# Seven products of a Strassen-Winograd matrix: three of them added up in PSUM, the relu moved to ScalarE, rstd applied behind the second matrix

## The reference, cut to what matters

```python
h = h + jnp.concatenate([y_rw, y_fox], axis=-1) @ w_out[i]
u = rmsnorm(h, norm_mlp[i])
h = h + jnp.square(jax.nn.relu(u @ w_ff1[i])) @ w_ff2[i]
gate = jax.nn.sigmoid(rmsnorm(h, norm_ple[i]) @ w_ple_gate[i])
```

## Time and profile before

| | us |
|---|---|
| median of 3 runs | 2773.17 (2772.51 to 2775.59) |
| the profiled execution | 2775.37 |
| its span, first to last instruction | 2773.8 |
| PE busy in the span | 2591.0 (93%) |
| VectorE | 1698.0 (61%) |
| ScalarE | 1031.7 (37%) |
| GpSimd | 565.3 (20%) |
| mean granted TensorE clock | 0.986 of full speed |

### The profile page before, as it was taken

The page is one execution under the profiler, slowest core; times in us unless marked ns, Lnnn a source line. Parts: engine busy times, 40 slices in busy tenths (PEclk is TensorE's granted clock), DMA queues, the critical chain, the costliest instruction groups (busy, mean ns, idle before and its releaser), DMA issues.

```text
span 2773.8 us, 48519 instructions
## 1 busy us (share of the span) xinstructions
PE 2591.0 (93%) x18322; PEld 2104.7 (76%) x18322; DVE 1698.0 (61%) x2030; ACT 1031.7 (37%) x1458; POOL 565.3 (20%) x389
## 2 busy tenths in 40 slices
PE   8999999999688998898999899879999999999998
PEld 5777777777577676677777777768888888888887
DVE  5565667666444645899999999973333333333443
ACT  4444444444455334333333333332222222233333
POOL 0000000000232025544444444410000000011010
PEclk9999999999899999999999999989999999999999
DMA  6555554555423334333333333364444444333333
GB/s 196 152 151 158 156 147 138 147 153 163 166 92 112 103 116 129 107 121 113 113 113 113 113 114 118 121 207 116 126 121 121 116 119 127 100 93 109 93 97 107
DMA packets 469436, 352.24 MB, mean 127 GB/s; under 512 B 56661, under 2 KB 435527, under 8 KB 468359
## 3 DMA queue, kind: packets, MB, share of 16 engines
q1 hardware_dynamic: 413111, 281.93, 35.1%
q0 software_dynamic: 11472, 39.43, 4.1%
q10 hardware_dynamic: 44800, 30.18, 3.3%
HBM read 294.21 MB, written 57.28 MB: 127 GB/s over the span
## 4 chain that ended last, share of the span: by engine, by line
issue 36%; PE 33%; DVE 20%; ACT 4%; POOL 3%; DMA 2%; SPq 1%; ACTq 1%; DVEq 0%; POOLq 0%
DVE w_lo L2296 8%; PE acc L682 7%; PE acc L684 6%; PE acc L683 6%; DVE tile_sums L2300 2%; DVE ev L2347 2%; PE bank L1188 2%; ACT w_hi L1285 1%; ACT w_hi L1677 1%; PE bank L1189 1%; DVE sq L2350 1%; POOL sumsq L2501 1%; PE bank L870 1%; POOL sumsq L2622 1%; ACT sq L1682 1%
## 5 line engine op out<-in xcount | busy, mean ns | idle before, releaser
L1815 DVE TENSOR_TENSOR w_lo<-w_raw,w_hi 128x1024 fp32r<-128x1024 f32 x292 | 361.2, 1237 | 760.9 <-ACT w_hi L1285 760.0
L1285 ACT ACTIVATE w_hi<-w_raw 128x1024 fp32r<-128x1024 f32 x292 | 308.7, 1057 | 791.3 <-PE acc L684 744.3
L1188 PE MATMUL bank<-mix,w_hi 128*128 128x512 f32 x1120 | 410.8, 405 | 62.1 <-DVE w_lo L2296 62.1
L682 PE MATMUL acc<-hidden,w_hi 128*128 128x512 f32 x1024 | 399.7, 390 | 15.6 <-DVE w_lo L1815 11.5
L684 PE MATMUL acc<-hidden,w_lo 128*128 128x512 f32 x1024 | 399.4, 390 | 0.0
L683 PE MATMUL acc<-hidden,w_hi 128*128 128x512 f32 x1024 | 399.3, 390 | 0.0
L682 PE MATMUL acc<-a_all,w_hi 128*128 128x512 f32 x800 | 321.7, 402 | 2.0 <-DVE w_lo L1815 2.0
L1189 PE MATMUL bank<-mix,w_lo 128*128 128x256 f32 x1120 | 314.9, 281 | 0.0
L684 PE MATMUL acc<-a_all,w_lo 128*128 128x512 f32 x800 | 313.1, 391 | 0.0
L683 PE MATMUL acc<-a_all,w_hi 128*128 128x512 f32 x800 | 312.8, 391 | 0.0
L1188 PEld LDWEIGHTS bank<-mix,w_hi 128*128 128x128 f32 x1120 | 212.2, 189 | 131.0 <-issue 49.7
(11 more groups left out here) (358 smaller groups left out, 4493.4 us busy)
## 6 DMA issues: line engine op xcount, KB each, us to landing
parts<-in_w_ff SPq DMA_DIRECT2D x64, 1024.0 KB, 5.8
w_raw<-in_w_ff SPq DMA_DIRECT2D x128, 512.0 KB, 3.9
w_raw<-in_w_in SPq DMA_DIRECT2D x100, 512.0 KB, 3.9
w_raw<-in_w_out SPq DMA_DIRECT2D x32, 512.0 KB, 4.0
hid_d<-sq ACTq DMA_DIRECT2D x32, 512.0 KB, 2.6
w_raw<-in_w_ple_gate SPq DMA_DIRECT2D x32, 512.0 KB, 4.0
z_d<-ev POOLq DMA_DIRECT2D x50, 256.0 KB, 3.4
ev<-hid_d SPq DMA_DIRECT2D x24, 512.0 KB, 4.5
```

What stands on the lines that cost most here:

```text
L682: mm(dst, wh, hi[kt], start=kt == 0, stop=False)
L1188: mm(dst[:, :], wh[:, j, :], mixed(u, j), start=j == 0, stop=False, skip_group_check=True)
L1285: A(w_hi[:, s, :, :], w_raw[:, s ^ raw_turned[0], :, :], ACT.Copy).then_inc(sg("w_hi_ready"), 1)
L1815: V.tensor_tensor(w_lo[:, s, :, 0:width], w_raw[:, s ^ raw_turned[0], :, 0:width], w_hi[:, s, :, 0:width].bitcast(F32), ALU.subtract).then ...
```

## The change

**PSUM.** The seven products keep their operands. Their order and their banks change. From pair 1 on: b11 into bank 0, b21 into bank 1, bt2 onto bank 0, bt1 into bank 2, bt3 onto bank 0, b22 onto bank 2, bt4 into bank 4. Before a product is added onto a bank, VectorE has read what stood there, since the partial sums are needed too. Pair 0 has a table of its own.

**VectorE.** Four reductions stay (`take_first`, `take_16`, `take_fifth`, `take_167`). The other three become two adds each that take a half of the bank straight from PSUM. Relu and rstd leave VectorE: ScalarE does the relu ahead of its square (`store_hidden`), and rstd, squared, multiplies the second matrix's result (`grow_second`, two instructions where `grow` was one).

**GpSimd and SP.** bt2 is made second and bt3 third; the two halves of the weights are loaded later in the pair than before.

**Seams.** In the output projection's loop ScalarE makes the high part of the weights ahead of scaling. GpSimd makes bt1 of pair 0 ahead of the last tile's sums. At the end SP loads the weights of the second matrix's tile 1 ahead of the wait for the last hidden store, and the second half of h is loaded two tiles later.

```diff
+
+    A11, A12, S2, S1, S3, S4, A22 = range(UNITS)
+    FIRST_PAIR = ((b11, A11, bank[0], True), (b21, A12, bank[1], True), (b22, S4, bank[2], True), (bt1, S1, bank[5], True),
+                  (bt2, S2, bank[0], False), (bt3, S3, acc[0], True), (bt4, A22, bank[4], True))
+    LATER_PAIR = ((b11, A11, bank[0], True), (b21, A12, bank[1], True), (bt2, S2, bank[0], False), (bt1, S1, bank[2], True),
+                  (bt3, S3, bank[0], False), (b22, S4, bank[2], False), (bt4, A22, bank[4], True))
+    LATER_TURN = (1, 2, 3, 0, 4, 5, 6)
+
+    def pair_order(p):
+
+        return FIRST_PAIR if p == 0 else LATER_PAIR
+
+    def turn_of(p, u):
+
+        return LATER_TURN[u] if p > 1 else u
 
     Z_ODD = 2
...
+                    sp.wait_ge(sg("weight_sums_made"), i * 4 + (past("weight_sums_made") + a + 3))
                     sp.sem_inc(sg("waits_taken"), 1)
-                    sp.wait_ge(sg("w_split"), i * UNITS + (FIRST + 2 * a + 3))
+                    sp.wait_ge(sg("w_split"), i * UNITS + (FIRST + 4 * a + 4))
...
             second_units(0, 0, 0)
             for q in range(4, UK):
                 load_staged(q)
-            sp.wait_ge(sg("relu_ready"), past("relu_ready") + PAIRS)
+            second_units(0, 0, 1)
+            sp.wait_ge(sg("hidden_relu"), past("hidden_relu") + PAIRS)
             sp.wait_ge(sg("hidden_stored"), past("hidden_stored") + 16 * PAIRS)
-            second_units(0, 0, 1)
             stage_hidden(1, 0)
...
+                    pe.wait_ge(sg("w_split"), i * UNITS + (FIRST + UNITS * p + max(turn_of(p, v) for v in range(u + 1)) + 3))
+                    if p == 0:
+                        if u == 4:
+                            pe.wait_ge(sg("products_taken"), past("products_taken") + 1)
+                        if u == 5:
+                            pe.wait_ge(sg("acc_taken"), M_FF + 1)
+                    elif u == 6:
+                        pe.wait_ge(sg("hidden_summed"), i + (past("hidden_summed") + p))
+                    else:
+                        pe.wait_ge(sg("products_taken"), i * 6 + (past("products_taken") + 6 * (p - 1) + (5, 2, 7, 6, 9, 10)[u]))
...
                             pe.wait_ge(sg("mix_split"), past("mix_split") + 3 * NJ + (2 if u == 2 else 3))
-                        mm(dst[:, :], wh[:, j, :], mixed(u, j), start=j == 0, stop=False, skip_group_check=True)
-                        last = mm(dst[:, 0:HT], wl[:, j, :], mixed(u, j)[:, 0:HT], start=False, stop=j == NJ, skip_group_check=True)
+                        mm(dst[:, :], wh[:, j, :], mixed(x, j), start=fresh and j == 0, stop=False, skip_group_check=True)
...
+                hi_unit(0, i, M_OUT + KT // 2 + 1, a_turn=1)
                 scale_tile(i, 0, 0)
                 square_tile(i, 0, 0)
-                hi_unit(0, i, M_OUT + KT // 2 + 1, a_turn=1)
+                hi_unit(1, i, M_OUT + KT // 2 + 1, a_turn=1)
...
+                if p == 0:
+                    act.wait_ge(sg("squares_summed"), 2 + 2 * KT)
                 else:
-                    freed = FIRST + 2 + UNITS * p + (u - 2 if u < 3 else u - 6 if u == 3 else u - 3)
-                act.wait_ge(sg("unit_done"), i * UNITS + freed)
-                A(slots[slot_of[u]][0], weights_of[u], ACT.Copy).then_inc(sg("w_hi_ready"), 1)
-
-            def square_hidden(i, p):
-
-                act.wait_ge(sg("relu_ready"), i + (past("relu_ready") + p + 1))
+                    act.wait_ge(sg("hidden_stored"), i * 16 + (past("hidden_stored") + 16 * p))
+                A(sq[:, :, :], ev[:, :, :], ACT.Relu).then_inc(sg("hidden_relu"), 1)
+                act.wait_ge(sg("hidden_relu"), i + (past("hidden_relu") + p + 1))
                 A(sq[:, :, :], sq[:, :, :], ACT.Square).then_inc(sg("hidden_squared"), 1)
                 act.wait_ge(sg("hidden_squared"), i + (past("hidden_squared") + p + 1))
                 act.dma_start(hid_d[bass.ds(i + p, 1), :, :, :].rearrange("a p b t -> (a p) b t"), sq[:, :, :]).then_inc(sg("hidden_stored"), 16)
...
+                lo_unit(1, i * 2 + (OUT_U + 3))
                 mix_los(i, 0, 0)
-                lo_unit(1, i * 2 + (OUT_U + 3))
...
-            def sums_76(i, p):
+                    V.reduce_sum(sum_167, halves_of(bank[0]), AX.X).then_inc(sg("products_taken"), 1)
...
-                take_product(pq[3], 4)
-                take_product(pq[4], 5).then_inc(sg("products_taken"), 1)
-                taken(i, p, 3)
-                then(V.tensor_tensor(pq[4], pq[0], pq[4], ALU.add))
-                V.tensor_tensor(ev[:, 1, 0:HT], pq[4], pq[1], ALU.add)
-                V.tensor_tensor(pq[3], pq[3], pq[4], ALU.add)
-
-            def sums_4(i, p):
+                then(V.tensor_tensor(ev[:, 1, 0:HT], bank[2][:, 0:HT], sum_16, ALU.add))
+                if p == 0:
+                    then(V.tensor_tensor(ev[:, 1, 0:HT], ev[:, 1, 0:HT], fifth, ALU.add))
+                V.tensor_tensor(ev[:, 1, 0:HT], bank[2][:, HT:T], ev[:, 1, 0:HT], ALU.add).then_inc(sg("products_taken"), 1)
+
+            def sum_21(i, p):
 
                 await_product(i, p, 6)
-                dve.wait_ge(sg("w_split"), i * UNITS + (FIRST + UNITS * (p + 1) + 1 + 3))
-                take_product(pq[1], 6).then_inc(sg("products_taken"), 1)
-                taken(i, p, 4)
-                then(V.tensor_tensor(ev[:, :, HT:T], pq[3][:, None, :].broadcast_to([P, 2, HT]), tile_sums[:, 1:3, :], ALU.add))
-                if p:
-                    dve.wait_ge(sg("hidden_stored"), i * 16 + (past("hidden_stored") + 16 * p))
-                V.scalar_tensor_tensor(sq[:, :, :], ev[:, :, :], 0.0, rstd[:, None, :].broadcast_to([P, 2, T]), ALU.max, ALU.mult).then_inc(
-                    sg("relu_ready"), 1)
+                then(V.tensor_tensor(ev[:, 0, HT:T], bank[4][:, 0:HT], sum_167, ALU.add))
+                V.tensor_tensor(ev[:, 0, HT:T], bank[4][:, HT:T], ev[:, 0, HT:T], ALU.add).then_inc(sg("hidden_summed"), 1)
+
+            def begin_pair(i, p):
+
+                take_first(i, p)
+                product_lo(i, p, 4)
+                sum_11(i, p)
+                product_lo(i, p, 5)
+                take_16(i, p, 3, 2)
+                product_lo(i, p, 6)
+                take_fifth(i, p, 3)
 
...
+            mean_square(1)
+            sum_21(0, 0)
+            product_lo(0, 1, 2)
+            product_lo(0, 1, 3)
+            invert_root(1)
+            begin_pair(0, 1)
+            then(V.tensor_tensor(rstd[:, :], rstd[:, :], rstd[:, :], ALU.mult))
             with dve.Fori(0, PAIRS - 2) as i:
-                end = chained(i, 2)
-                sums_35(i, 1)
+                end = chained(i, 3)
+                product_lo(i, 2, 3)
+                take_167(i, 1, 4)
+                sum_22(i, 1)
                 product_lo(i, 2, 0)
-                sums_76(i, 1)
+                sum_12(i, 1)
                 product_lo(i, 2, 1)
-                to_last_lo(i, 2, lambda: sums_4(i, 1))
+                sum_21(i, 1)
+                product_lo(i, 2, 2)
+                begin_pair(i, 2)
...
+            def grow_second(i, b, n):
+
+                V.tensor_tensor(grown_part[:, b, :], acc[b][:, :], rstd[:, :], ALU.mult).then_inc(sg("acc_taken"), 1)
+                dve.wait_ge(sg("acc_taken"), 2 * i + (n + b + 3))
+                return V.tensor_tensor(h2[:, bass.ds(2 * i + b, 1), :], h2[:, bass.ds(2 * i + b, 1), :], grown_part[:, b:b + 1, :], ALU.add)
...
             pool.wait_ge(sg("unit_done"), FIRST + 2 + UNITS * PAIRS)
             for n in range(2):
+                if n:
+                    pool.wait_ge(sg("unit_done"), FIRST + 2 + UNITS * PAIRS + 4)
```

More of the change, by code:

```diff
@@ L385, in build @@
     slot_of = (0, 1, 2, 3, 0, 1, 2)
[L386 to L388 removed]
+    b11, b12, b21, b22 = parts[:, 0, :, 0:P], parts[:, 0, :, P:], parts[:, 1, :, 0:P], parts[:, 1, :, P:]
+    bt1, bt2, bt3, bt4 = (tsum[:, n, :, :] for n in range(4))
+    A11, A12, S2, S1, S3, S4, A22 = range(UNITS)
[8 more added lines that the diff above has]
+        return LATER_TURN[u] if p > 1 else u
     Z_ODD = 2
```

274 lines of the change are left out of this document (141 added, 133 removed).

## The result

The changed kernel takes 2714.14 us (median of 4 runs, 2709.24 to 2714.75); the kernel before, run between them, 2774.38. The ratio is 0.9778, 95% interval 0.9761 to 0.9795: faster by 60 us, where 109 were forecast.

| stretch | before, us | after, us | difference | forecast |
|---|---|---|---|---|
| to the projection's last matmul | 1106.93 | 1091.21 | -15.7 | -14.5 |
| from there to the last step of pair 1 | 58.13 | 64.54 | +6.4 | -5.5 |
| the other 30 pairs | 676.4 (22.55 a pair) | 636.8 (21.23) | -39.6 | -72.6 |
| from there to the end | 932.3 | 920.7 | -11.7 | -16 |

What follows compares the result with a forecast made beforehand. VectorE, 98.5% busy, was taken to set the pace, PE some 3 us behind. Terms -14.5 - 5.5 - 71.6 - 1 - 16 = -108.6 took the profiled 2775.4 to 2666.8, as median 2664.6; prediction 2665, range 2645 to 2706.

Steps and rivals of the forecast that it cites:

- The pairs: Loop over column-tile pairs of the first MLP matrix: 20.1 us a pair instead of 22.57, saving 71.6 us.
- PE's floor: First MLP matrix: seven products of 2.78 us need 19.5 us a pair on PE.
- rival 2: Loop over pairs: PE alone sets the pace, 19.5 us a pair, a further -17, kernel 2647; chance 0.20.
- the 0.6 us wait at product 6: Loop over pairs: PE waits once a pair, at product 6, for the third reduction, losing 0.6 us.
- VectorE's work: Loop over pairs: VectorE's work falls from 16.2 to 13.2 us a pair, its port-bound part from 11.6 to 8.3.
- Rival 1: Loop over pairs: GpSimd keeps the port over back-to-back sums 2 and 3; 21.45 us a pair, kernel 2704; chance 0.20.
- Projection: Output projection: ScalarE's high part of the weights goes first, removing PE's waits; -14.5 us.
- Start: First two pairs after the projection: early sum 1 lets product 4 start sooner; -5.5 us, bounds 0 and -12.
- Seam: Passage to the second matrix: tile 1's weight loads issued before the last store's wait; -16 us, bounds -8 and -18.

Runs made afterwards that it cites:

- x2: Changed kernel with one wait more: GpSimd's sum 2 of a pair waits for the low part of that pair's product 1; 2703.7 us, ratio 0.9741.
- x3: Changed kernel with VectorE's add of two SBUF inputs (sum of a22) moved behind the low part of the next pair's product 1; 2710.4 us, ratio 0.9766.
- x9: Changed kernel with b11's low and high parts (product 1) ahead of bt1's (product 4) in the loop over the pairs; 2674.8 us, ratio 0.9646.
- x4: Changed kernel with the order of the output projection's loop restored on ScalarE and VectorE; 2728.8 us, ratio 0.9824.
- x1: Changed kernel with the second reciprocal and the squaring of rstd moved behind the loop over the pairs; 2710.7 us, ratio 0.9764.
- x11: x9 plus x1's change, with pair 1's low part for product 4 behind the reduction that product 3 waits for; 2667.9 us, ratio 0.9620.
- x7: Changed kernel with the first pair's sum 1 back behind the last tile's sums on GpSimd; 2720.0 us, ratio 0.9793.
- x13: x11 with VectorE's wait for h moved from ahead of the second matrix's loop to the add that uses it; 2671.1 us, ratio 0.9633.
- x5: Changed kernel with the loads for tile 1 of the second matrix behind the last relu and store waits again; 2723.2 us, ratio 0.9814.

## Why the prediction was wrong, step by step

**The pairs: the step that failed.** The prediction placed one pair and had it close at 20.1 us; it measured 21.23. It closed with "low part 1 to 17.75" and "sum 2 gets the port at 17.75". It also had the weights for sum 2 land at 16.35, under the add that lasts to 16.6, and low part 1 ask only at 16.6: sum 2 had asked first, and I gave the port to the other all the same. The trace follows the placing to 0.5 us up to there and then decides it the other way. With product 1 starting at 1177.2, sum 1 starts at 10.7 (placed 10.25), sum 2 is released and runs at 16.6 (16.35), low part 1 asks at 16.7 and waits (16.6). What repeats is two pairs, one short (19.0 to 20.2) and one long (22.8 to 23.9). x2 shows that the alternation goes when the add and low part 1 are both ahead of sum 2, x3 that low part 1 alone is not enough; x9 shows that the loss goes altogether when VectorE's queue no longer holds product 1's part behind product 4's. That order stood in the diff, and I placed "low part 4 of the next pair" ahead of low part 1 without asking what it holds up when it is late. It is late where sum 1 is: with the order at the port fixed (x2) sum 1 runs at 13.1 of its pair (1436.34, product 1 from 1423.3) and not at 10.25. Its load is asked for at 5.5, behind a sum 3 that I had done by 3.6, and lands 7.4 us later, where I took 5.8.

**PE's floor: a term mis-sized.** I took 2.78 us a product from the earlier trace rows, hence 19.5. Most undisturbed products take 2.83, in the changed kernel's loop (110 of 173) as in before's (74 of 121), and a pair of them 19.79; rival 2's 19.5 was never to be had at that pace. Over the 30 pairs that is 9 us, and the 0.6 us wait at product 6 would have stood on top of it. There was no such wait: PE waits at products 1, 2, 3 and 5.

**VectorE's work** was right in size: the adds with a PSUM operand take 0.41 to 0.43 us and are never stretched, reductions 0.68 to 0.69. The group rows of 1200 to 1780 us, to be held against the earlier trace rows:

```profile
L2328 DVE TENSOR_TENSOR w_lo<-parts,w_hi 128x1024 fp32r<-128x1024 f32 x82 | 162.5, 1981 | 3.2 <-ACT w_hi L1699 3.2
L2381 DVE TENSOR_TENSOR ev<-tile_sums 128x256 f32<-128x256 f32 x27 | 27.3, 1010 | 0.9
...
L2394 DVE TENSOR_TENSOR ev<-bank,tile_sums 128x256 f32<-128x256 f32 x28 | 11.5, 412 | 0.0
```

The one 256-wide add without a PSUM operand (L2381) takes 1010 ns on average, its equal from PSUM 412. By the Trainium skill (SBUF — State Buffer, "Who interferes with whom") VectorE's instructions contend with GpSimd's reads if they have two SBUF inputs and, outside the two-port modes, not if they have one at most. The trace agrees.

**Rival 1** came close in size (21.45 a pair, 2704) and not in kind: GpSimd did not keep the port over two sums. In every long pair one instruction of VectorE got in between sums 2 and 3, in five of them a low part as in the first one shown above, in eight the add L2381, after which the low part was held by sum 3 (1409.17, 3.39 us). That the number fits rival 1 is luck.

**Projection:** right, -15.7 for -14.5 (x4). **Start:** wrong by 12 us. I priced the reciprocal's wait at 4 us and it was 7.8, with the low part ahead of it held as well (x1, x11). Product 4 was placed 14.3 us behind the projection's end and started after 19.3, hardly earlier than the 19.8 before. The early sum 1 was ready at 1093.8, but the low part of bt1 stands in VectorE's queue behind the last `mix_los`, which sum 2 held (1103.44, 3.36 us), and was itself held by sum 3 (1107.07, 3.37 us); and the early sum costs 2.3 us at product 1, where I had it collide with nothing (x7). The 3.8 us of the reciprocal and the 5.0 of product 4 are 9 of the 12 us; the rest is not isolated. **Seam:** -11.7 for -16. The wait that the trace names is h's, beside the staged tiles, 3.1 us plus the lower clock, where I had left 2.5. x13, without the wait for h in that place, is no shorter, so h is not alone in it, and x5 prices the moved loads at 2 to 6 us where I had taken the whole wait of 11.5.
